# Expert rows of the first group joined in pairs: a scaled row and a multiply-add in the ring in place of two diagonal matmuls

## What is computed

```python
def one(xs):                                   # 128 tokens
    q = (xs @ wq).reshape(PEER_BLOCK, PEER_HEADS, 2, PEER_HALF)
    s1 = jnp.einsum('nhd,hkd->nhk', q[:, :, 0], keys[0])
    s2 = jnp.einsum('nhd,hkd->nhk', q[:, :, 1], keys[1])
    ...                                        # top 16 of each, top 16 of their 256 sums
    g = jax.nn.softmax(top, axis=-1)
    a = jax.nn.gelu(jnp.einsum('nd,nhjd->nhj', xs, u[eid]), approximate=False)
    return jnp.einsum('nhj,nhjd->nd', g * a, v[eid])
```

## Time and profile before

| | us |
|---|---|
| runs, median of 3 (lowest to highest) | 3469.24 (3466.94 to 3478.2) |
| span of the profiled execution, first to last instruction | 3470.7 |
| TensorE busy (share) | 2832.0 (82%) |
| VectorE busy | 1722.3 (50%) |
| ScalarE busy | 1109.9 (32%) |
| GpSimd busy | 874.4 (25%) |
| moved by the transfer engines | 1071.87 MB, mean 309 GB/s |

### The profile page before, as it was taken

One profiled execution on the slowest core, in us unless ns is written; L12 is line 12 of the kernel. 1 busy time (PEld: TensorE's weight loads), 2 busy tenths in 40 slices (PEclk: granted clock), 3 DMA queues, 4 the chain that ended last, 5 costly groups with the idle time before them and its releaser, 6 DMA issues.

```text
span 3470.7 us, 42239 instructions
## 1 busy us (share of the span) xinstructions
PE 2832.0 (82%) x16102; PEld 1777.9 (51%) x16102; DVE 1722.3 (50%) x4262; ACT 1109.9 (32%) x3213; POOL 874.4 (25%) x772
## 2 busy tenths in 40 slices
PE   7999999989988999988775655699999985655555
PEld 6787887645555666664431111277788851211111
DVE  1322003557676555446676666422301266667665
ACT  2222102243664454323533223232310123333222
POOL 0000000233333333223334444200000034444443
PEclk9999999999998999999997677699999998886777
DMA  9663442989998999969999999732144199999998
GB/s 374 242 237 130 156 152 88 386 329 378 388 364 325 410 411 420 380 262 375 400 378 416 400 405 417 316 122 85 62 157 151 74 365 401 416 415 408 411 410 339
DMA packets 151785, 1071.87 MB, mean 309 GB/s; under 512 B 16668, under 2 KB 19356, under 8 KB 23200
## 3 DMA queue, kind: packets, MB, share of 16 engines
q0 software_dynamic: 110592, 805.36, 57.3%
q1 hardware_dynamic: 40992, 263.82, 19.8%
HBM read 1068.06 MB, written 1.05 MB: 308 GB/s over the span
## 4 chain that ended last, share of the span: by engine, by line
PE 50%; DMA 27%; DVE 11%; ACT 6%; issue 3%; POOL 2%; SPq 0%; POOLq 0%; DVEq 0%; ACTq 0%
PE bank L410 37%; DMA ring<-in_experts,eid 26%; PE bank L424 10%; DVE ring L1442 5%; POOL ring L1884 2%; ACT topk_work L958 1%; ACT topk_work L951 1%; PE bank L517 1%; DMA ring<-in_quads 1%; ACT topk_work L948 1%; PE bank L437 1%; ACT L948 1%; DVE state L1649 1%; PE bank L641 0%; DVE topk_work L1412 0%
## 5 line engine op out<-in xcount | busy, mean ns | idle before, releaser
L1884 POOL DMA_INDIRECT ring<-in_experts,eid x768 | 874.2, 1138 | 2570.8 <-PE bank L424 1260.2
L424 PE MATMUL bank<-ring,topk_work 64*64 64x512 f32 x6144 | 969.1, 759 | 562.6 <-ACT topk_work L958 555.7
L1442 DVE CUSTOM_DVE_ANT_0 ring<-ring,h2tok 128x1024 f32<-128x1024 f32 x768 | 937.1, 1225 | 592.6 <-DMA ring<-in_experts,eid 589.3
L424 PEld LDWEIGHTS bank<-ring,topk_work 64*64 64x64 f32 x6144 | 233.9, 157 | 1184.6 <-ACT topk_work L958 894.9
L948 ACT ACTIVATE topk_work<-topk_work 128x2 f32<-128x2 f32 x384 | 78.0, 203 | 1147.9 <-DVE topk_work L1442 1147.3
L410 PE MATMUL bank<-h_even,weights 128*128 128x256 f32 (+1 forms) x1312 | 297.8, 385 | 5.5 <-ACT h_even L1031 4.0
L410 PEld LDWEIGHTS bank<-h_even,weights 128*128 128x128 f32 (+1 forms) x1312 | 246.3, 190 | 60.7 <-issue 22.0
L410 PE MATMUL bank<-h_odd,weights 128*128 128x256 f32 (+1 forms) x1040 | 235.9, 383 | 0.0
L958 ACT ACTIVATE topk_work<-const,topk_work 128x64 f32<-128x64 f32 x768 | 225.7, 341 | 0.2 <-ACT topk_work L951 0.2
L410 PEld LDWEIGHTS bank<-h_odd,weights 128*128 128x128 f32 (+1 forms) x1040 | 193.9, 189 | 51.9 <-issue 24.1
L951 ACT ACTIVATE topk_work<-topk_work 128x1 f32<-128x1 f32 x768 | 184.6, 287 | 12.6
(11 more groups left out here) (246 smaller groups left out, 3091.8 us busy)
## 6 DMA issues: line engine op xcount, KB each, us to landing
weights<-in_quads SPq DMA_DIRECT2D x150, 1024.0 KB, 8.8
ring<-in_quads SPq DMA_DIRECT2D x85, 1024.0 KB, 4.8
ring<-in_experts,eid POOLq DMA_INDIRECT x768, 9.2
ring<-in_quads SPq DMA_DIRECT2D x6, 768.0 KB, 4.3
weights<-in_quads SPq DMA_DIRECT2D x6, 768.0 KB, 7.5
weights<-in_quads SPq DMA_DIRECT2D x12, 256.0 KB
xT<-in_xT SPq DMA_DIRECT2D x2, 1024.0 KB, 11.0
out<-state SPq DMA_DIRECT2D x4, 256.0 KB, 5.0
```

Source lines behind the costliest of these rows:

```text
L424: x = nc.tensor.matmul(acc[g][out, :], diag[mine, J % 4, :], ring[mine, J % RING, D + h * 512:D + (h + 1) * 512], start=first, stop=J % TI ...
L1442: v.tensor_tensor_reduce(row, row, h2tok[:, u // UNITS % 2, :], 1.0, 0.0, ALU.mult, ALU.add, dots[:, u % 2, j:j + 1]).then_inc(S["dot_done ...
L1884: pool.indirect_dma_start(ring[:, J % RING, :], None, d["experts"], bass.IndirectOffsetOnAxis(eid[:, u % 2, j:j + 1], 0)).then_inc(gathere ...
```

## The change

The rows of group 0 alone are treated differently (`joined(n)` is true for n < 128). For a pair of them ScalarE makes no diagonals. It scales the v half of the pair's first row in its ring slot with that row's weight (128x1024, in place). VectorE then adds the second row's v half, times its weight, to it, again in place (`scalar_tensor_tensor`, 128x1024, `join_until`). TensorE multiplies the constant 64-column identity with this one row: four matmuls per pair in place of eight. Both ring slots of the pair are given back together afterwards.

On VectorE the sum of pair n stands behind the first dot of pair n + 1, or, where TensorE needs it earlier by the plan, in front of the next copy. Four weights buffers (`gelw`) are in use, so ScalarE's gelu of pair n waits until the sum of pair n - 4 is done. The model's time for a row of group 0 becomes 0.475.

```diff
@@ -57,6 +57,7 @@
 BANKS = 6
+JOINED = 1
 FIXED, EXTRA = 3, 4
...
@@ -311,6 +312,14 @@
             return g * GROUP_PAIRS
+        def joined(n):
+            return n < JOINED * GROUP_PAIRS
+        def diags(J):
+            return J - JOINED * GROUP_ROWS
@@ -409,14 +418,33 @@
+            def joined_pair(n):
+                k, first, last = n // TILE_PAIRS, n % TILE_PAIRS == 0, n % TILE_PAIRS == TILE_PAIRS - 1
+                if first and n:
+                    for g in range(2):
+                        pe.wait_ge(*at("evicted", "acc", k - 1, g))
+                pe.wait_ge(S["pair_ready"], n + 1)
+                for h in range(2):
+                    out = slice(h * BLK, (h + 1) * BLK)
+                    for g in range(2):
+                        mine = slice(g * BLK, (g + 1) * BLK)
+                        x = nc.tensor.matmul(acc[g][out, :], ident_blk[mine, :],
+                                             ring[mine, 2 * n % RING, D + h * 512:D + (h + 1) * 512],
+                                             start=first, stop=last, skip_group_check=True)
+                x.then_inc(S["row_used"], 2)
             def row_pair(n):
+                if joined(n):
+                    joined_pair(n)
+                    return
                 for J in (2 * n, 2 * n + 1):
-                    pe.wait_ge(S["diag_ready"], J + 1)
+                    pe.wait_ge(S["diag_ready"], diags(J) + 1)
                     for h in range(2):
@@ -449,7 +477,7 @@
                 for J in (2 * n, 2 * n + 1):
-                    plan.now += 0.95
+                    plan.now += 0.475 if joined(n) else 0.95
                     if (J + RING) // GROUP_ROWS == J // GROUP_ROWS:
@@ -943,6 +971,9 @@
                 m = n % 4 * 2
+                if n >= 4 and joined(n - 4):
+                    act.wait_ge(S["pair_ready"], n - 3)
@@ -950,13 +981,19 @@
                                          scale=wts[:, par, j + c:j + c + 1]).then_inc(S["act_gelu"], 1)
-                if J >= 4:
-
-                    act.wait_ge(S["row_used"], J - 2)
-                for c in range(2):
-                    act.wait_ge(S["act_gelu"], 3 * n + 2 + c)
-                    nc.scalar.activation(diag[:, (J + c) % 4, :], ident_blk, ACT.Copy,
-                                         scale=gelw[:, m + c:m + c + 1]).then_inc(S["diag_ready"], 1)
+                if joined(n):
+                    act.wait_ge(S["act_gelu"], 3 * n + 2)
+                    row = ring[:, J % RING, D:2 * D]
+                    nc.scalar.activation(row, row, ACT.Copy, scale=gelw[:, m:m + 1]).then_inc(S["row_scaled"], 1)
+                else:
+                    if diags(J) >= 4:
+                        act.wait_ge(S["row_used"], J - 2)
+                    for c in range(2):
+                        act.wait_ge(S["act_gelu"], 3 * n + 2 + c)
+                        nc.scalar.activation(diag[:, (J + c) % 4, :], ident_blk, ACT.Copy,
+                                             scale=gelw[:, m + c:m + c + 1]).then_inc(S["diag_ready"], 1)
                 if j == 4 and u + 1 < GROUPS * 2 * UNITS and (u + 1) not in LEADS:
...
@@ -1413,8 +1450,10 @@
                     step(v.tensor_scalar(eidf, chosen[:, 0:PTOP], float(PK), float(i * N_EXP), ALU.mult, ALU.add), u, "eidf")
-                    if u:
-                        dve.wait_ge(S["diag_ready"], (u - 1) * PTOP)
+                    if u > 1 and joined((u - 1) * UNIT_PAIRS - 1):
+                        dve.wait_ge(S["pair_ready"], (u - 1) * UNIT_PAIRS)
+                    elif u > 1:
+                        dve.wait_ge(S["diag_ready"], diags((u - 1) * PTOP))
                     settled(u, "eidf")
@@ -1441,10 +1480,13 @@
                                            dots[:, u % 2, j:j + 1]).then_inc(S["dot_done"], 1)
+                    join_until(n)
                     if u + 1 < GROUPS * 2 * UNITS and (u + 1) not in LEADS:
                             choose(u + 1, 2 * j + 1)
+                if joined(n) and not joined(n + 1):
+                    join_until(n + 1)
                 if n % TILE_PAIRS == 0 and n // TILE_PAIRS in (1, 2, 3):
@@ -1453,6 +1495,17 @@
                     last_norm(0)
+            def join_until(n):
+                while cur["joined"] < min(n, JOINED * GROUP_PAIRS):
+                    J, m = 2 * cur["joined"], cur["joined"] % 4 * 2
+                    dve.wait_ge(S["row_scaled"], cur["joined"] + 1)
+                    dve.wait_ge(S["act_gelu"], 3 * cur["joined"] + 3)
+                    row = ring[:, J % RING, D:2 * D]
+                    v.scalar_tensor_tensor(out=row, in0=ring[:, (J + 1) % RING, D:2 * D], scalar=gelw[:, m + 1:m + 2],
+                                           in1=row, op0=ALU.mult, op1=ALU.add).then_inc(S["pair_ready"], 1)
+                    cur["joined"] += 1
@@ -1510,6 +1563,8 @@
                     rows_until(n + 1)
+                while cur["joined"] < cur["next"] and joined(cur["joined"]) and placed[cur["joined"]][0] <= now:
+                    join_until(cur["joined"] + 1)
```

More of the change, by code:

```diff
@@ L270, in build @@
                   "eids_ready", "shift_ready", "exp_ready", "wts_ready", "dot_done", "act_gelu", "diag_ready",
-                  "row_used"):
+                  "row_used", "row_scaled", "pair_ready"):
             sem(n)
@@ L1336, in _ @@
             v = nc.vector
-            cur = {"next": 0, "limit": 0}
+            cur = {"next": 0, "limit": 0, "joined": 0}
             def copy_out(out, b, *key):
```

## The result

| | before | after |
|---|---|---|
| time, median of 4 runs each (lowest to highest), us | 3468.09 (3457.75 to 3478.20) | 3671.52 (3658.05 to 3673.41) |
| span of the profiled execution, us | 3470.7 | 3669.2 |
| TensorE busy, us | 2832.0 | 2795.9 |
| VectorE busy, us | 1722.3 | 1872.6 |
| ScalarE busy, us | 1109.9 | 1156.7 |

The ratio is 1.058 (95% interval 1.055 to 1.060): 203 us slower, far outside the forecast range of 3438 to 3500. The last two rows of the table are read from the timeline; they are called the stage and the gap from here on. The stage got 228 us longer, the gap 23 us shorter. Together that is 205 us. The spans differ by 198.5: the first gather comes 1.8 us earlier, and all behind the first gather of group 1 takes 1956 us for 1961, so nothing to explain lies there.

A forecast was written before the change was run, and what follows sets the result against it. Group 0's stage was taken as bound by a six-row ring, neither TensorE nor transfers alone, within 69 us of the transfers' need. -24 + 5 + 2 + 4 + 14 + 5 - 4 = +2: 3471 us, no change; range 3438 to 3500.

The forecast's parts named there:

- The ring must bear a longer hold: Six-row ring in group 0's stage: slots held about 3 us longer, leaving 7 us for a gather; price 0.
- is bound by transfers with and without the change: Planner's order: a cheaper pair brings no rows forward; fewer pairs stand beside each projection, the rest at the end.
- its end (+2, +4): Last block of pairs: 52 rows running alone cost +2 us, VectorE's two units with choosing +4 (0 to 7).
- the gap, 24 us: Last landing of group 0 to first gather of group 1: 17 us instead of 41.4, a gain of 24.
- The block: Last 26 pairs in one block: 2.57 us per row; slots held about 9.5 of 15.4 us, leaving just enough.
- the mark of 2.7: Sign for VectorE as the bound: block rows landing slower than 2.7 us each; the other sign, sums idling long for ScalarE.
- rival 3: VectorE becomes the bound; sums queued behind the next dot make TensorE wait, ring full: +27 us, 3496 us; chance 0.26.
- The attentions: Fewer pairs beside the latent attention cost +14 us (+3 to +20), beside the linear attention +5 (0 to 15).
- The operations: Per pair: VectorE's sum 1.22 us (0.69 to 1.38), ScalarE's scaling 1.03 us (0.62 to 1.24).
- TensorE -120: TensorE's busy time falls by about 120 us: 128 joined pairs, each 0.94 us less.
- Ports: Gathers on GpSimd beside VectorE's two-input instructions: loss per gather 0.3 us instead of 0.2, adding nothing to the sum.
- Rivals 1 and 2: TensorE's relief shortens the attentions: 3452 us, chance 0.22; it also frees slots, a third of 69 us back: 3429, 0.08.

The follow-up runs named there:

- five-slot run: Kernel before, with GpSimd's gathers of group 0 waiting for one slot more, so only five of six ring slots are in use: 3535.0 us (+65).
- 8-column runs: Changed kernel with the sum cut to 8 of 1024 columns: 3574.0 us; scaling cut too: 3545.8 us; both cut and planner's lag at 8 us: 3511.4 us.
- e1_small_sum: Changed kernel with VectorE's sum cut to 8 of its 1024 columns, its place and waits kept: 3574.0 us (+109).
- e2_small_both: Changed kernel with VectorE's sum and ScalarE's scaling both cut to 8 columns: 3545.8 us (+81).
- g1_before_extra_dve: Kernel before, with one unused 976-column reduction added on VectorE behind the dots of each of group 0's 128 pairs: 3495.9 us (+31).

## Why the prediction was wrong

- **Failed: "The ring must bear a longer hold ... so the transfers stay full: price 0."** This step carries most of the error, 165 of 203 us in the order of adding above. The hold was forecast 3 us longer and became some 8 us longer; of six slots' turn, 25.8 us, only 7.9 are from issue to landing. I had taken the lengths of the added operations and one dot, and subtracted TensorE's saving, but no wait for a turn on ScalarE's and VectorE's queues behind other work. And I had read the room in a turn from 1100:1460 alone, where the transfers are full, with a landing time (10.1 us) that is the whole stage's. Nor had I priced that the planner's lag of 5 us was made for the shorter chain: TensorE's weight loads waited 365 us for sums, where they had waited 96 for diagonals. The five-slot run shows that the ring had no such room over the whole stage (+65 us for one slot); the 8-column runs and the lag show the chain (43 + 28 + 94 us, of which a later place gives 83 back).
- **Wrong in kind: the plan "is bound by transfers with and without the change".** The planner's cost of a pair isn't a price but decides how many pairs stand beside each product. The block of left-over pairs that I saw in the order was the sign of it. I priced its end (+2, +4) but not that the projections now had too few rows beside them: +38 us, as measured in the kernel before.
- **Right in size, wrong in meaning: the gap, 24 us.** It fell from 41.4 to 18.3 us (17 was forecast). But it is no gain: with the low cost for the last pairs alone, or with the lag at 6.5 us, it fell just so and the time did not move. The queries' products that left it stand ahead of the last dot.
- **The block.** Forecast were 2.57 us per row and a hold "just enough". It ran at 3.1 (32 gathers in 1550:1650), with TensorE at its low clock (0.50) and busy for only 32 of 100 us; unjoined rows in such a block ran at 2.5 (low cost in the kernel before). That passes the mark of 2.7 that I had set for rival 3, and the other sign set for it came too: over the stage VectorE's sums stood 81 us for ScalarE, though only 0.9 us of it in the block.
- **The attentions.** Forecast +14 and +5. The share fell from 0.89 to 0.66 in the stretch 746:862 (the work in it is not quite the same). The latent attention itself, from its first to its last maximum, took 95 us for 97. The 32 pairs joined at the end of the group, in neither attention, cost 33 us; so the loss is not the attentions' alone, and the question of which engine paces them, to which most of my working went, was not the one that mattered. The loss isn't even, though: rows 64 to 95 lost the most, 63 us, of which 29 come with the low cost alone; why there is open.
- **The operations** were sized within 10%: 1281 for 1220 ns, 1132 for 1030. ScalarE +47 and VectorE +150 us of busy time came as forecast.
- **TensorE -120** came as -36: a joined pair took more than half of a pair of before (1.09 us for 0.94 at the full clock), and the clock was lower. And the relief bought nothing that the longer chain didn't take back: the kernel with both operations on 8 columns has TensorE busy for 760 us up to the next group, the kernel before with the low cost alone 851, and the former is 43 us slower; at a lag of 8 the two are level (+37 and +37). The Trainium skill (Trainium Kernel Development and Optimization, "Performance Expectations") takes the weight loads' share, not the matmuls', as the measure of how close TensorE is to its limit. By that it had room already, and these runs agree.
- **Ports.** Priced at nothing, rightly: a gather's mean on GpSimd is 1102 ns for 1138, with 128 more two-input instructions on VectorE. The Trainium skill (GPSIMD Engine Reference, "1. Specifications") names contention with VectorE's instructions that have two SBUF inputs. Single gathers agree: in the stage after, all 128 that started with VectorE idle took 0.93 to 0.95 us, and 56 of the 76 that started beside a dot or a sum took over 1.2, up to 1.97. But the mean did not rise, so it is no cost of the sum.
- **The rivals.** Rival 3 had the right sign and mechanism in its half sentence "queued behind the next dot, then makes TensorE wait with the ring full", but tied it to VectorE being full and priced it at 27 us. 148 us of plain load on VectorE cost 31 us, near that price; the chain and the order were the rest. Rivals 1 and 2 (TensorE's relief) are refuted. No rival came within 170 us of the result, so the chances given to them say little.

What stays open: how much of the chain's cost is ScalarE standing at an eviction and how much VectorE's order. Putting the sum right behind the pair's own dots could have told it. It was not run; by a reading of the orders alone, the engines would then wait for each other for ever. Open too is the joined kernel at the planner's old cost. No version with joined pairs that was run reached the kernel before (the nearest, 32 pairs, is 33 us slower), and none of the changes to its planner beat it.

## What to carry to other kernels

- Where buffers in a small ring set the pace, price a change by what it does to the time from a buffer's filling to its return, each in-order queue on the way with what stands in front. Work off that chain cost 0.2 us for each us here; on it 0.7, or 0.35 where the order left the chain more time.
- Test the ring's room before relying on it: take one slot away in the kernel before. If that costs time, no hold is free.
- A cost in a planner is a knob of the order, not a price. Change it alone first; halving it cost 38 us here and raising it by a quarter 56. When a change makes a chain longer, ask which lag in the plan was made for the old length: 3 us more gave back 83 of 203 us. And a shorter gap counts only with the start of what follows it: read the next gather's time, not the idle time before it.

## What the runs showed of the hardware

- The clock's feedback. As TensorE waited more, its granted clock from the first gather to the next group's fell from 0.96 to 0.83, and the same products (2460 and 2474 of their records) took 608 for 569 us. In the block (1550:1650 of the kernel after), where it stood most, it was at 0.50, the lower of its two levels (1.2 GHz).
- A tensor-by-scalar-plus-tensor of 1024 columns on VectorE takes 1281 ns (kernel after) and 224 ns on 8 columns (e1_small_sum); a scaled copy on ScalarE 1132 (kernel after) and 285 ns (e2_small_both).
- The issue of a gather on GpSimd takes 0.94 us with VectorE idle and up to 1.97 beside one of its two-input instructions of 1024 columns (kernel after, the stage); beside its copies, maxima and the reduction of g1_before_extra_dve, which have one input, it stays at 0.94.
